# The last modulation's gate summed on VectorE among the attention layer's weight units

## The reference, cut to what matters

```python
sc, scc = silu(c), silu(c_ctx)                     # one row of 2048 each
for i in range(2):
    shift, scale, gate    = split(sc  @ mod_w[i] + mod_b[i], 3)   # latent tokens
    cshift, cscale, cgate = split(scc @ mod_w[i] + mod_b[i], 3)   # context tokens
    h_lat = rms_norm(x, g[i])   * (1 + scale)  + shift
    h_ctx = rms_norm(ctx, g[i]) * (1 + cscale) + cshift
    y_lat, y_ctx = mixer(h_lat, h_ctx)
    x = x + gate * y_lat
    if i == 0: ctx = ctx + cgate * y_ctx
```

## Time and profile before

| what | value |
|---|---|
| median of 3 runs | 2595.79 us (2592.61 to 2597.37) |
| the profiled execution | 2592.13 us |
| its span, first to last instruction | 2590.3 us |
| mean granted TensorE clock | 0.990 of full speed |
| PE busy | 2509.2 us (97%) |
| DVE busy | 1444.5 us (56%) |
| ACT busy | 1178.6 us (46%) |

### The profile page before, as it was taken

One profiled execution on the slowest core, in us unless ns is written; L12 is line 12 of the kernel. 1 busy time (PEld: TensorE's weight loads), 2 busy tenths in 40 slices (PEclk: granted clock), 3 DMA queues, 4 the chain that ended last, 5 costly groups with the idle time before them and its releaser, 6 DMA issues.

```text
span 2590.3 us, 31456 instructions
## 1 busy us (share of the span) xinstructions
PE 2509.2 (97%) x12080; PEld 1958.0 (76%) x12080; DVE 1444.5 (56%) x1905; ACT 1178.6 (46%) x1727; POOL 259.2 (10%) x138
## 2 busy tenths in 40 slices
PE   6999999999999999999999999899899999999978
PEld 5887777777777667788777777787787877878767
DVE  4644444544545455566767676635545474654764
ACT  6444334553444434456565655424425344253542
POOL 0000000000000000002555554001200000000000
PEclk9999999999999999999999999999999999999999
DMA  6568777736787888865333333324334243342323
GB/s 218 179 187 271 239 240 249 245 106 217 240 278 265 268 288 280 282 230 147 98 93 97 93 93 92 107 82 146 114 98 136 84 122 98 97 130 85 123 86 130
DMA packets 277298, 429.42 MB, mean 166 GB/s; under 512 B 14502, under 2 KB 93116, under 8 KB 276028
## 3 DMA queue, kind: packets, MB, share of 16 engines
q1 hardware_dynamic: 275772, 422.28, 51.4%
q10 hardware_dynamic: 1408, 5.51, 0.6%
HBM read 425.64 MB, written 2.10 MB: 165 GB/s over the span
## 4 chain that ended last, share of the span: by engine, by line
PE 89%; DVE 4%; ACT 4%; issue 1%; DMA 1%; SPq 0%; ACTq 0%; DVEq 0%
PE ps L725 62%; PE ps L1106 13%; PE ps L798 4%; PE ps L1089 2%; ACT ring_hi L1332 1%; PE ps L876 1%; PE ps L903 1%; PE ps L1212 1%; PE ps L1230 1%; PE ps L776 1%; PE ps L1061 1%; DVE ring_lo L1794 1%; PE ps L809 1%; PE ps L888 1%; ACT second_block L1689 0%
## 5 line engine op out<-in xcount | busy, mean ns | idle before, releaser
L1332 ACT CAST ring_hi<-ring 128x1024 fp32r<-128x1024 f32 (+2 forms) x598 | 619.6, 1039 | 1044.5 <-PE ps L725 598.7
L1794 DVE TENSOR_TENSOR ring_lo<-ring,ring_hi 128x1024 fp32r<-128x1024 f32 (+2 forms) x522 | 629.2, 1212 | 793.9 <-ACT ring_hi L1332 791.4
L725 PE MATMUL ps<-ring_hi,act_hi 128*128 128x512 f32 (+2 forms) x1272 | 513.6, 404 | 9.9 <-issue 4.4
L725 PE MATMUL ps<-ring_hi,act_lo 128*128 128x512 f32 (+2 forms) x1272 | 493.4, 388 | 0.0
L725 PE MATMUL ps<-ring_lo,act_hi 128*128 128x512 f32 (+2 forms) x1272 | 491.6, 386 | 0.0
L725 PE MATMUL ps<-ring_hi,features_hi 128*128 128x512 f32 x1152 | 462.4, 401 | 15.1 <-DVE features_lo L2230 7.4
L725 PE MATMUL ps<-ring_hi,features_lo 128*128 128x512 f32 x1152 | 452.5, 393 | 0.0
L725 PE MATMUL ps<-ring_lo,features_hi 128*128 128x512 f32 x1152 | 452.3, 393 | 0.0
L725 PEld LDWEIGHTS ps<-ring_hi,act_hi 128*128 128x128 f32 x1272 | 240.3, 189 | 112.2 <-issue 47.2
L725 PEld LDWEIGHTS ps<-ring_hi,features_hi 128*128 128x128 f32 x1152 | 218.8, 190 | 84.7 <-issue 27.2
L725 PEld LDWEIGHTS ps<-ring_hi,act_lo 128*128 128x128 f32 x1272 | 239.9, 189 | 51.1
(11 more groups left out here) (246 smaller groups left out, 2417.7 us busy)
## 6 DMA issues: line engine op xcount, KB each, us to landing
ring<-in_mod_w SPq DMA_DIRECT2D x192, 512.0 KB, 5.1
ring<-in_att_w_in SPq DMA_DIRECT2D x128, 512.0 KB, 3.7
ring<-in_ev_w_in SPq DMA_DIRECT2D x104, 512.0 KB, 4.8
ring<-in_od_w_in SPq DMA_DIRECT2D x96, 512.0 KB, 5.5
ring<-in_lru_w_in SPq DMA_DIRECT2D x64, 512.0 KB, 4.1
ring<-in_ev_w_out SPq DMA_DIRECT2D x40, 512.0 KB, 4.8
ring<-in_lru_w_out SPq DMA_DIRECT2D x40, 512.0 KB, 3.7
ring<-in_od_w_out SPq DMA_DIRECT2D x36, 512.0 KB, 4.5
```

The source lines that it names most:

```text
L725: mm = pe.matmul(PS[:, bank, 0:n], a, w[:, k - k0, :], start=(k == k_first and j == 0), stop=(k == k_last and j == 2))
L1332: act.copy(high(U, n), raw(U, n)).then_inc(s_hi, 1)
L1794: dve.tensor_tensor(out=low(U, n), in0=raw(U, n), in1=high(U, n).bitcast(F32), op=ALU.subtract).then_inc(s_lo, 1)
```

## The change

The gate of the last layer's modulation (4 chunks, 32 mod units) leaves the odd layer. 20 mod chunks are left, and gaps 1 of the odd turns hold one pair fewer, gaps 3 of the four turns DIL 0 to 2 and MEM 0 none. The 32 units are loaded in the last layer instead, one (`gate_mod`) behind every fourth `att_in` unit, so that the ring order has 40 units a group. PE doesn't multiply them. DVE does, for the latent row only: `gate_mod(i, g)` multiplies the unit's two 128 x 512 blocks by a per-partition scalar of `cond_t` and adds them to two 128 x 512 accumulators (`GACC`, in a part of the buffer of the last group's outputs). In head step s = 1 of each group PE adds the accumulators up over the partitions (8 matmuls, one column each, by a column of ones), and DVE adds the bias (`gate_columns`). New waits keep this in order: PE's multiplication of the third ring unit behind a gate unit waits for `gate_mod_step`, and SP, where the slot to be refilled held a gate unit, waits until that third unit has been multiplied, not for the slot's own unit. The gate unit is counted as used together with the unit ahead of it.

```diff
-N_MOD = 24
+N_MOD = 20
-MOD_CHUNK = [(0, m) for m in range(10)] + [(1, 11)] + [(1, m) for m in range(11)] + [(0, 10), (0, 11)]
+MOD_CHUNK = [(0, m) for m in range(12)] + [(1, m) for m in range(8)]
...
-OD_TURNS = lay_turns(10, [(SWA[j], i, (1, 3, 2, 1), (0, 2, 1, 1)) for j in range(2) for i in range(4)]
+OD_TURNS = lay_turns(10, [(SWA[j], i, (1, 3, 2, 1), (0, 1, 1, 1)) for j in range(2) for i in range(4)]
...
-    _queue([(_stage, u) for u in range(_n)])
+    for _u in range(_n):
+        _queue([(_stage, _u)])
+        if _stage == "att_in" and _u % 4 == 3:
+            _queue([("gate_mod", _u // 4)])
...
+ATT_RING, ATT_SPLIT = 40, 32
+GATE_TAKEN = 3
+def used_by(U):
+    return 2 if U + 1 < len(RING) and RING[U + 1][0] == "gate_mod" else 1
...
                 if U + per >= SLOTS:
-                    sp.wait_ge(*raw_free(U + per - SLOTS, i, per, 1 if per else 0))
+                    back = U + per - SLOTS
+                    sp.wait_ge(*raw_free(back + (GATE_TAKEN if RING[back][0] == "gate_mod" else 0), i, per, 1 if per else 0))
...
                 split_ready(U, i, per)
+                stage, g = RING[U - GATE_TAKEN] if U >= GATE_TAKEN else (None, 0)
+                if stage == "gate_mod":
+                    pe.wait_ge(s_gm, at(2 * g + 2, i, 16))
...
-                mm.then_inc(s_wused, 1)
+                mm.then_inc(s_wused, used_by(U))
...
+                if s == 1:
+                    pe.wait_ge(s_gm, i * 16 + 16)
+                    for k in range(4):
+                        for half in range(2):
+                            mm = pe.matmul(PS[:, 7, 2 * P + k:2 * P + k + 1], GACC[:, half, k * P:(k + 1) * P], SEL[:, 2:3],
+                                           start=(half == 0), stop=(half == 1))
                 mm.then_inc(s_e11, 1)
...
+            def gate_mod(i, g):
+                fixed = isinstance(i, int)
+                U = POS["gate_mod", 8 * (i + 1 if fixed else 1) + g]
...
+                for k in range(2 * g, 2 * g + 2):
+                    rows, by = raw(U)[:, k % 2 * CHUNK:(k % 2 + 1) * CHUNK], CS[:, 2 * k:2 * k + 1]
+                    acc, before = GACC[:, k % 2, :], 16 * (i + 1) + k if fixed else i * 16 + (16 + k)
+                    if k < 2:
+                        ins = dve.tensor_scalar(acc, rows, by, None, ALU.mult)
+                    else:
+                        dve.wait_ge(s_gm, before - 1)
+                        ins = dve.scalar_tensor_tensor(out=acc, in0=rows, scalar=by, in1=acc, op0=ALU.mult, op1=ALU.add)
+                    ins.then_inc(s_gm, 1)
...
                 att_lo(i, [24])
+                gate_mod(i, 4)
                 qk_gain(link)
...
                 for u in range(28, 32):
                     att_lo(i, [u])
+                    if u in (28, 31):
+                        gate_mod(i, 5 + (u == 31))
...
+                gate_mod(i, 7)
...
                     output(i, s)
+                    if s % 2:
+                        gate_mod(i, s // 2)
```

More of the change, by code:

```diff
@@ L296 @@
     SPLIT_BEFORE.append(sum(_made))
-    if _name == "mod":
+    if _name in ("mod", "gate_mod"):
         LO_BY.append(None)
@@ L304, with att_at @@
 AHEAD = 5
+ATT_RING, ATT_SPLIT = 40, 32
+GATE_TAKEN = 3
+def att_at(i, u):
+    n = ATT_SPLIT * ((i if isinstance(i, int) else 0) + 1) + u
+    return POS["att_in", n] if n < ATT_SPLIT * GROUPS else POS["att_out", n - ATT_SPLIT * GROUPS]
+def used_by(U):
+    return 2 if U + 1 < len(RING) and RING[U + 1][0] == "gate_mod" else 1
 def split_behind(U):
@@ L690, in att_units @@
                     for u in range(8):
-                        unit(UNIT0["att_in"] + j * 8 + u, t["att_w_in_2"][0], u * 2, 2, j * D if i is None else i * CHUNK + j * D,
-                             CHUNK, i, 32)
+                        n = j * 8 + u
+                        unit(POS["att_in", n], t["att_w_in_2"][0], u * 2, 2, j * D if i is None else i * CHUNK + j * D,
+                             CHUNK, i, ATT_RING)
+                        if n % 4 == 3:
+                            unit(POS["gate_mod", n // 4], t["mod_w_2"][1], n // 4 * 2, 2, 2 * D if i is None else i * CHUNK + 2 * D,
+                                 CHUNK, i, ATT_RING)
             att_units()
@@ L808, in sum_mod @@
                 for j in range(4):
-                    mm = pe.matmul(PS[:, bank, 2 * j:2 * j + 2], rows[:, j * P:(j + 1) * P], SEL[:], start=True, stop=True)
+                    mm = pe.matmul(PS[:, bank, 2 * j:2 * j + 2], rows[:, j * P:(j + 1) * P], SEL[:, 0:2], start=True, stop=True)
                 mm.then_inc(s_modt, 1)
@@ L1335, in his @@
                 for u in units:
-                    hi(UNIT0[stage] + u, n, i, per)
+                    hi(UNIT0[stage] + u if i is not None else POS[stage, u], n, i, per)
             made = [0]
@@ L1776, in _ @@
             y_hi(2 * OUT_AHEAD, KT - 2 * OUT_AHEAD, DYH, DYT)
-            with act.Fori(2, 4) as i:
-                his("att_out", range(8), i=i, per=8)
+            with act.Fori(0, 2) as i:
+                his("att_out", range(16, 24), i=i, per=8)
         @block.vector
@@ L1798, in los @@
                 for u in units:
-                    if i is not None or not LO_BY[UNIT0[stage] + u][0]:
-                        lo(UNIT0[stage] + u, n, i, per)
+                    U = UNIT0[stage] + u if i is not None else POS[stage, u]
+                    if i is not None or not LO_BY[U][0]:
+                        lo(U, n, i, per)
             made = [0]
@@ L2448, in _ @@
                 split_features(part(FTH, 0), part(FTL, 0), TMP_B, 2 * j, 2)
-            att_lo(-1, range(12, 20))
+            gate_mod(-1, 1)
+            att_lo(-1, range(12, 16))
+            gate_mod(-1, 2)
+            att_lo(-1, range(16, 20))
+            gate_mod(-1, 3)
             projections_behind(-1, False)
```

47 lines of the change are left out of this document (34 added, 13 removed).

## The result

The changed kernel takes 2682.1 us in the median (2680.35 to 2686.76, 4 runs), the kernel before 2594.2 us beside it (2590.03 to 2597.37, 4 runs): ratio 1.0344, 95% interval 1.0325 to 1.0362. That is 88 us slower, where 44 was forecast. The profiled execution spans 2678.7 us, 88.4 more than that of before.

The account below looks back on a forecast made before the run. PE, busy 97% of the span, was taken to bound the kernel. Terms of -20.8 + 10.4 + 18.3 + 20.8 + 3 + 2.5 + 3 + 6.8 gave +44.0 us on 2592.1, forecast 2636 us, range 2600 to 2658.

Parts of the forecast that it names:

- The odd layer, -20.8: Odd layer: 16 pairs of mod units and four chunk sums leave a full PE, saving 20.8 us.
- Rival 4: Odd layer gains only 10 us, DMA or softmax being next in line: 2647 us; chance 0.70 together with the forecast.
- Waits for gate steps ahead of units 22 and 26, +10.4: Last layer: PE waits for DVE's gate steps, 0.9 us and 1.7 us, in four groups: +10.4 us.
- Head steps, +18.3: Head steps 1 to 3: late casts and gate columns delay PE 6.1 us a group, in three groups: +18.3 us.
- Transitions, +20.8: Behind unit 30: late cast of unit 2 and a gate step cost 5.2 us at each of four transitions.
- Lead-in, +3: Lead-in: late cast of unit 10 delays the scaled features that PE already waits for: +3 us.
- The end, +2.5: Last group: gate columns, 1.6 us, and att_out unit 7 late by about 1: +2.5 us.
- Landing, +3: Bursts of four loads: first lands near 3.7 us, with 0.3 us added at 11 places: +3 us.
- The clock, +6.8: PE's clock falls after stalls: 1.7 us counted once at each of four transitions, partly hidden in head steps: +6.8 us.
- rivals, 3: Slower than forecast: landing at 5.5 us and clock low after every stall, +71 us, 2663 us; chance 0.08.

Follow-up runs that it names:

- early_refill: Changed kernel, but SP waits for DVE's gate step itself before refilling a gate unit's slot, and PE's waits for gate steps are gone: 2590.33 us.
- dve_only: Changed kernel without gate units in the ring, mod_w loads in the last layer or late refill; DVE's operations, columns and PE's waits stay: 2597.12 us.
- late_dve: dve_only plus the late refill of every fourth att_in slot, still without gate units in the ring or mod_w loads: 2672.19 us.
- late_one: Kernel before, with SP's late refill at att_in unit 2 of each group alone: 2613.66 us.
- odd_only: Changed kernel with its odd layer only: 20 modulation chunks, nothing of the gate in the last layer: 2571.89 us.
- late_heads: Kernel before, with SP's late refill at att_in units 6 and 10 alone, in head steps 1 and 3: 2614.37 us.

## Why the prediction was right or wrong

The direction and the mechanism were right: undoing the late refill, and with it PE's waits for gate steps (`early_refill`), takes back all of the loss. The size was half of what was measured, and the time lies above the range. By the forecast's own steps:

1. **The odd layer, -20.8.** Right: -21.9, PE full in it. Rival 4 (a gain of 10) falls.
2. **Waits for gate steps ahead of units 22 and 26, +10.4.** The term that failed first. PE waits 4.45, 4.28, 4.50 and 4.39 us ahead of unit 22 (0.9 forecast) and 3.22, 2.74, 2.42 and 2.87 ahead of unit 26 (1.7 forecast): 28.9 in all, the page's number. The 0.9 and 1.7 were read from the timeline of before, as if the casts came as early as there; `dve_only`, where they do, has 0.5 to 0.6 and 1.3 to 1.6. But the next term of the same prediction said that those casts come late. The two were added, never put into one timeline.
3. **Head steps, +18.3.** 28.9 by the trace, in three groups. Steps 1 and 3 are longer by 2.4 and 2.3 us, as forecast (2.4 each). Step 2 is longer by 4.6, not 1.3. The columns behind the stall take 1.9 us, and the clock is low for 6.8 us, which is 3.4 us. `dve_only` has the columns and no low clock, and its step is longer by 1.5; `late_dve` has both, and 4.6. That steps with 24 matmuls cover the late casts was right (52.9 to 53.0).
4. **Transitions, +20.8.** Near: PE's waits at the four transitions are 23.5 us in all, 17.5 more than before. That `late_one` costs 19.2 where its forecast had 22 is in part luck. Its late cast stands at three transitions, not four, with 3.3 us of new waits (3.8 forecast) and 6.8 us of low clock (3.4 forecast) at each: 3 x 6.7 = 20.1.
5. **Lead-in, +3.** Nearly nothing: PE waits 8.14 us where it waited 5.17, but a stall of 2.46 us just ahead of it is gone.
6. **The end, +2.5.** 5.6 by the traces (last heads 60.1 us for 53.8, the rest 0.7 shorter). PE's idle time in those heads is 7.8 us for 7.6; the columns and a clock low for 10.2 us make it up.
7. **Landing, +3.** The median went from 3.7 to 4.7 us. The forecast looked at the first load of a burst only. The second lands 4.7 us behind its issue, the fourth 7.1 (medians of the last layer's bursts); in `late_dve`, which has no `mod_w` in its bursts, the fourth 6.3. That fits the 8 us of the gate's loads.
8. **The clock, +6.8.** The largest error. The mean granted clock is 0.976 of 2678.7 us for 0.990 of 2590.3; the low stretches, halved, are 64.5 us for 25.4, so it costs up to 39 us. PE's busy time says nearly the same: 2532.2 us, 44.9 more than the 2487.3 of `odd_only`, of which the columns are 7.6. The forecast charged 1.7 us once a transition. The low stretch behind a stall was 3.4 us in the earlier trace rows, and mostly 6.8 in the changed kernel, and head steps have it too. The sentence that part of it hides behind the loop over DVE had no row, and `late_heads` shows it wrong: behind five of its six stalls the next step is longer too, by 1.3 to 1.7 us.

With the clock's part of 3 (10.2 us) and 6 (5.1) counted under 8 alone, these terms make up some 105 of the last layer's 110 us; about 5 have no place. The errors of 2 (18.5 us) and 8 (32) are more than the 44 that were missed; 4, 5 and 6 go the other way by 2 to 3 us each. Of the rivals, 3 ("landing at 5.5 and the clock low after every stall", 2663) named the clock and priced it at 10 more. The Trainium skill, "TensorE: Matmul & The Clock Gate", section on HAM oscillation, told of this: short runs of matmuls between DMA waits, each starting at the lower clock. The trace agrees (0.50 for 6.8 us behind the stall in head step 1), though not at every stall (behind the one of 2.28 us in head step 1 of `late_heads`' group 2 the clock stays full), and charging each stall by it was nearer than the forecast's own choice, though still too little at 1.7 us each.

What stays open: whether the first group's waits, which in the changed kernel hold loads there though no gate unit lay in the slot, cost anything, and how much of the 92 us each of the things is worth that `early_refill` undoes at once. No run tells these apart.

## What to carry to other kernels

When a shared ring of buffers gets a unit of another kind, ask what releases its slot and what waits behind that in the queue that loads: a wait for a stand-in (here "three units later on PE") turns loads that lead into loads that are waited for, in bursts, while the averages still look half idle. Let the loader wait for the true last reader, and put that reader early and where the full engine's units are long. And price two delays of one chain in one timeline: a step that costs 0.5 us of waiting in the old schedule cost 4.3 to 4.5 when what it stands behind came some 4 us late.

## What the runs showed of the hardware

A stall on PE cost its length and half the low stretch of the clock behind it, which was 3.4 or 6.8 us: the six stalls of 2.2 to 2.5 us in `late_heads` made steps 0 to 7 of its three groups longer by 7.8, 8.1 and 6.5 us, 3.7 a stall in the mean. It isn't a fixed price: the group with 6.5 has one stall with no low stretch behind it. The last group's heads have the same instructions in the kernel before and in `late_one`, and PE is idle 7.6 and 7.8 us in them. Windows of before and of `late_one`:

```profile
2458.40:2512.20 53.80, 46.16 (x229) 33.53 (x228) 32.32 (x59) 21.90 (x42) 0.00 (x0) 1.00 0.31 102
```

```profile
2482.90:2539.60 56.70, 48.94 (x230) 35.29 (x228) 32.58 (x60) 22.17 (x42) 0.00 (x0) 0.94 0.30 96
```

The one keeps the full clock through its waits of 2 us, the other has 0.94 and takes 2.9 us longer. What tips it isn't in these traces.

The averages of DMA mislead too. The DMA view of the changed kernel, 32 us in 40 slices (busy share in tenths, GB/s):

```profile
DMA  0005799999989300000000000000000088999999
GB/s 0 0 0 84 207 387 410 376 376 392 348 207 361 128 20 0 0 0 0 0 0 0 0 0 0 0 0 0 0 0 0 0 131 246 392 410 374 387 384 351
```

Five loads, mostly at 350 to 410 GB/s, then nothing for some 13 us. The mean share of the last layer's window, 0.32, is below that of before, 0.36, and yet the casts wait for this queue 201.6 us.
